# A two-layer SSD/HGRN2/PEER trunk on one core: queries projected before their norm's root is known, and the final norm taken on token rows

## The reference

```
def rmsnorm(x, g):
    r = lax.rsqrt(jnp.mean(xf * xf, axis=-1, keepdims=True) + NORM_EPS)
    return (xf * r).astype(x.dtype) * g

for layer in range(DEPTH):                      # DEPTH = 2
    h = rmsnorm(x, mix_norm_g[layer])
    x = x + (ssd_mixer if layer == 0 else hgrn2_mixer)(h, ...)
    h = rmsnorm(x, ffn_norm_g[layer])
    x = x + peer_ffn(h, w_query, sub_keys, u, v)
return rmsnorm(x, final_norm_g)

# peer_ffn: q = h @ w_query (2048 columns); scores q . sub_keys; top 16 of each half,
# top 16 of their sums, softmax gates; out = sum over chosen experts of gate * gelu(h . u) * v
```

## Time and profile before

| | |
|---|---|
| median of three runs | 2242.07 us |
| profiled execution, its own time | 2241.06 us |
| its span | 2239.3 us |
| PE busy | 2111.5 us (94%) |
| ACT, DVE, POOL busy | 1105.0, 1126.4, 1160.8 us |
| mean granted clock of PE | 0.98 |

### The profile page before, as it was taken

One profiled execution on the slowest core, in us unless ns is written; L12 is line 12 of the kernel. 1 busy time (PEld: TensorE's weight loads), 2 busy tenths in 40 slices (PEclk: granted clock), 3 DMA queues, 4 the chain that ended last, 5 costly groups with the idle time before them and its releaser, 6 DMA issues.

```text
span 2239.3 us, 42069 instructions
## 1 busy us (share of the span) xinstructions
PE 2111.5 (94%) x14527; PEld 1942.0 (87%) x14530; DVE 1126.4 (50%) x1760; ACT 1105.0 (49%) x1693; POOL 1160.8 (52%) x584
## 2 busy tenths in 40 slices
PE   6987799999999999999988988999999999999998
PEld 5986799999999878888878978999999987888886
DVE  5867419990002854444445841899200086444444
ACT  4654354445445655545445444544454465454553
POOL 0162568898885044554520006799888703545552
PEclk9998999999999999999999989999999999999999
DMA  4531445555563055565533334555566404555552
GB/s 144 165 122 50 150 150 169 178 168 194 184 197 110 1 188 192 193 194 192 194 130 132 114 105 132 158 168 167 181 196 197 159 1 134 195 190 194 193 193 102
DMA packets 103887, 345.71 MB, mean 154 GB/s; under 512 B 18704, under 2 KB 20240, under 8 KB 103440
## 3 DMA queue, kind: packets, MB, share of 16 engines
q1 hardware_dynamic: 94512, 340.67, 46.5%
q10 hardware_dynamic: 9312, 4.19, 1.0%
HBM read 341.68 MB, written 3.15 MB: 154 GB/s over the span
## 4 chain that ended last, share of the span: by engine, by line
PE 48%; issue 30%; POOL 20%; DVE 1%; POOLq 0%; ACT 0%; DVEq 0%; ACTq 0%
PE banks L1076 31%; POOL wlo L411 20%; PE banks L748 10%; PE banks L1056 6%; PE banks L1037 1%; POOLq L410 0%; POOLq L415 0%; PE banks L791 0%; DVE x L1644 0%; DVE big L1110 0%; DVE big L1639 0%; DVE big L1609 0%; POOL hlo L440 0%; DVE raw L1618 0%; POOL big L425 0%
## 5 line engine op out<-in xcount | busy, mean ns | idle before, releaser
L411 POOL TENSOR_TENSOR wlo<-raw,whi 128x1024 fp32r<-128x1024 f32 x320 | 805.1, 2522 | 535.2 <-ACT whi L452 534.3
L748 PE MATMUL banks<-hhi,whi 128*128 128x256 f32 x3072 | 882.2, 287 | 62.9 <-DVE hlo L1120 26.4
L748 PE MATMUL banks<-hlo,whi 128*128 128x256 f32 x3072 | 875.7, 285 | 0.0
L748 PE MATMUL banks<-hhi,wlo 128*128 128x256 f32 x3072 | 875.1, 285 | 0.0
L452 ACT ACTIVATE whi<-raw 128x1024 fp32r<-128x1024 f32 x640 | 675.6, 1056 | 388.4 <-PE banks L1076 339.3
L748 PEld LDWEIGHTS banks<-hhi,whi 128*128 128x128 f32 x3072 | 596.1, 194 | 71.0 <-issue 48.3
L440 POOL TENSOR_TENSOR hlo<-big,hhi 128x256 fp32r<-128x256 f32 x256 | 351.7, 1374 | 505.9 <-ACT hhi L712 505.9
L748 PEld LDWEIGHTS banks<-hlo,whi 128*128 128x128 f32 x3072 | 596.4, 194 | 0.1
L748 PEld LDWEIGHTS banks<-hhi,wlo 128*128 128x128 f32 x3072 | 596.0, 194 | 0.0
L1632 DVE TENSOR_TENSOR wlo<-raw,whi 128x1024 fp32r<-128x1024 f32 x256 | 315.5, 1233 | 371.5 <-ACT whi L452 371.5
L1076 PE MATMUL banks<-whi,hhi 128*128 128x512 f32 x1024 | 316.8, 391 | 4.5 <-POOL hlo L440 4.5
(11 more groups left out here) (237 smaller groups left out, 1354.0 us busy)
## 6 DMA issues: line engine op xcount, KB each, us to landing
raw<-w_u SPq DMA_DIRECT2D x256, 512.0 KB, 3.5
raw<-w_v SPq DMA_DIRECT2D x256, 512.0 KB, 3.5
raw<-w_ssd_in SPq DMA_DIRECT2D x40, 512.0 KB, 3.5
raw<-w_q SPq DMA_DIRECT2D x32, 512.0 KB, 3.5
raw<-w_hgrn_in SPq DMA_DIRECT2D x32, 512.0 KB, 3.5
raw<-w_ssd_out SPq DMA_DIRECT2D x16, 512.0 KB, 3.5
raw<-w_hgrn_out SPq DMA_DIRECT2D x8, 512.0 KB, 3.5
big<-keys SPq DMA_DIRECT2D x2, 1024.0 KB, 7.5
```

The source lines that it names most:

```text
L411: nc.gpsimd.tensor_tensor(wlo[:, r, :, :], raw[:, r, :, :], whi[:, r, :, :].bitcast(F32), ALU.subtract).then_inc(lo_pool, 1)
L748: ins = nc.tensor.matmul(out, w[:, r, k, :], h[:, k, :], start=start and n == 0, stop=stop and n == 3 * KC - 1, **kw)
```

## The change

1. Queries. The first operand of q is no longer the normed hn: ACT makes hhi = g·x (scaled_hi, eight instructions of 256 columns) and DVE hlo = g·x − hhi (scaled_lo, eight), both without the root. PE computes q tiles 0 and 1, then the mean of the squares (norm), then the other tiles. DVE takes each q tile out of its bank with a multiplication by rstd, in place of ACT's copy, and makes hn (norm_scale) in between, one block each at tiles 4 to 11; ACT and DVE split hn at the end of q, for u. In layer 0 the additions of the mixer's output (add_acc) are interleaved with scaled_lo. The norm's PSUM bank of layer 0 moves from 3 to 7.
2. Value products. In contract the products with hhi of both token blocks come first, then, behind the wait for clo, those with hlo.
3. Final norm. In layer 1 clear() is replaced by 16 matmuls that put x, transposed, into banks 4 to 7, so that the value products are added to it. After v1 the squares and their sums over a row are taken from the banks (three of the four by ACT with an accumulator, one by DVE), the root is one number per partition, ACT and DVE scale the rows while they copy them to vt, PE transposes, and ACT and DVE apply g into fin, which four DMAs of 256 KB store.

```
+            def scaled_hi(n, ready, values):
+                for k in range(KC):
+                    if k % 2 == 0:
+                        act.wait_ge(ready, values[k // 2])
+                    nc.scalar.activation(hhi[:, k, :], x[:, k, :], ACT.Identity,
+                                         scale=par_at("norm_g", n * KC + k)).then_inc(hhi_done, 1)
...
+                act.wait_ge(mm_done, FIRST[f"q{layer}"])
+                scaled_hi(1 + 2 * layer, *ready)
+                for t in range(COUNT[f"q{layer}"]):
+                    hi(FIRST[f"q{layer}"] + t + 2, (t + 2) % RAW)
+                    if t == 1:
+                        squares(*ready)
+                        root(1 + 2 * layer)
+                act.wait_ge(mm_done, FIRST[f"u{layer}"])
                 acts_hi(hn, hn_done, 4 * layer + 3, 4 * layer + 4)
-                stream(f"q{layer}", copy_to(lambda t: col(t + SCRATCH0)))
...
+                project(f"q{layer}", 0, rs=range(2))
                 norm(1 + 2 * layer)
-                project(f"q{layer}")
+                project(f"q{layer}", 0, rs=range(2, RAW))
+                project(f"q{layer}", 1)
...
-                clear()
+                if layer == 0:
+                    clear()
+                else:
+                    for b in range(NB):
+                        for k in range(KC):
+                            nc.tensor.matmul(bank[4 + 2 * b + k // 4][:, P * (k % 4):P * (k % 4 + 1)],
+                                             x[:, k, b * P:(b + 1) * P], ident[:, :], start=k % 4 == 0, stop=True,
+                                             skip_group_check=True)
...
+            dve.wait_ge(mm_done, FIRST["q0"])
+            add_acc(0)
+            for b in range(4):
+                if b < 3:
+                    add_acc(b + 1)
+                scaled_lo(1, "q0", range(2 * b, 2 * b + 2))
...
+                norm_root(1 + 2 * layer)
+                for t in range(COUNT[f"q{layer}"]):
+                    dve.wait_ge(mm_done, FIRST[f"q{layer}"] + t + 1)
+                    nc.vector.tensor_tensor(q_t[:, t, :], bank[t % BANKS][:, 0:T], rstd[:, :],
+                                            ALU.mult).then_inc(evac, 1)
+                    if 4 <= t < 4 + KC:
+                        norm_scale(1 + 2 * layer, [t - 4])
+                acts_lo(hn, f"u{layer}")
...
+            for n in range(3):
+                b, e = divmod(n, 2)
+                nc.scalar.activation(fsq[:, b, 512 * e:512 * (e + 1)], bank[4 + n][:, :], ACT.Square,
+                                     accum_out=ssq[:, b, e:e + 1]).then_inc(fin_sq, 1)
             nc.scalar.preload_act_table(ACT.Sqrt)
-            norm(4, x_done, range(9, 13))
+            act.wait_ge(fin_ms, 1)
+            nc.scalar.activation(frs, frs, ACT.Sqrt).then_inc(fin_sd, 1)
+            act.wait_ge(fin_rs, 1)
+            for e in range(2):
+                nc.scalar.activation(vt[:, 0, 512 * e:512 * (e + 1)], bank[4 + e][:, :], ACT.Identity,
+                                     scale=frs[:, 0:1]).then_inc(fin_a, 1)
```

More of the change, by code:

```diff
@@ L85, with filled @@
 NCON = 3 + len(LEVELS)
-ACTS = {"ssd_in": 1, "y0": 2, "y1": 3, "q0": 4, "hgrn_in": 5, "hgrn_out": 6, "q1": 7}
+FILL = {}
+_at = 0
+for _n, _c in [("ssd_in", 2), ("y0", 2), ("y1", 2), ("q0", 8), ("u0", 2), ("hgrn_in", 2), ("hgrn_out", 2),
+               ("q1", 8), ("u1", 2)]:
+    FILL[_n] = _at, _c
+    _at += _c
+def filled(name, k=KC - 1):
+    at, n = FILL[name]
+    return at + k * n // KC + 1
 SCRATCH0 = 72
@@ L479, in col, with squares @@
                 return big[:, bass.ds(t, 1), :].rearrange("p a b -> p (a b)")
-            def norm(n, ready, values):
+            def squares(ready, values):
                 for b in range(4):
@@ L1069, in contract @@
                         pe.wait_ge(chi, 128 * layer + RAW * i + r + 1)
-                        pe.wait_ge(clo, 128 * layer + RAW * i + r + 1)
-                        for b in range(NB):
-                            tok = slice(b * P, (b + 1) * P)
-                            for c, ws in ((hhi, (whi, wlo)), (hlo, (whi,))):
+                        for c, ws in ((hhi, (whi, wlo)), (hlo, (whi,))):
+                            if c is hlo:
+                                pe.wait_ge(clo, 128 * layer + RAW * i + r + 1)
+                            for b in range(NB):
+                                tok = slice(b * P, (b + 1) * P)
                                 for w in ws:
@@ L1081, in _ @@
                     contract(i)
-                for b in range(NB):
-                    pe.wait_ge(vt_c, NB * layer + b + 1)
+                if layer == 0:
+                    for b in range(NB):
+                        pe.wait_ge(vt_c, b + 1)
                 for n in range(4):
+                    if layer == 1 and n % 2 == 0:
+                        pe.wait_ge(fin_a, n // 2 + 1)
+                        pe.wait_ge(fin_v, n // 2 + 1)
                     for j in range(2):
@@ L1102, in step, with norm_root @@
                 dve.wait_ge(own, count[0])
-            def norm(n, split=True):
+            def norm_root(n):
                 dve.wait_ge(ms_done, n + 1)
@@ L1108, in norm, with norm_scale @@
                 step(nc.vector.reciprocal(rstd[:, :], rstd[:, :]))
-                for k in range(KC):
+            def norm_scale(n, ks=range(KC)):
+                for k in ks:
                     ins = nc.vector.scalar_tensor_tensor(out=hn[:, k, :], in0=x[:, k, :],
@@ L1646, in _ @@
-            norm(4)
+                if layer == 0:
+                    for e in range(2):
+                        ins = nc.vector.tensor_copy(vt[:, 0, 512 * e:512 * (e + 1)], bank[4 + e][:, :])
+                    ins.then_inc(vt_c, 1)
+                    for n in range(4):
+                        dve.wait_ge(vt_mm, n + 1)
+                        v = x[:, 2 * n:2 * n + 2, :]
+                        nc.vector.tensor_tensor(v, v, bank[n][:, :].rearrange("p (m t) -> p m t", m=2),
+                                                ALU.add).then_inc(x_done, 1)
```

122 lines of the change are left out of this document (80 added, 42 removed).

## The result

The changed kernel takes 2216.0 us (median of 4 runs, 2214.3 to 2216.1), the kernel before 2239.7 (median of 4, 2237.2 to 2243.4). The ratio is 0.9894, 95% interval [0.9881, 0.9906]: 23.7 us less, faster. Four more runs of the changed kernel later gave 2215.5 to 2219.5, with the ratio 0.9893 [0.9878, 0.9908].

What follows compares the result with a forecast made beforehand. PE bounds the kernel, busy 2111.5 of 2239.3 us, so waits can win about 128. Terms 6.2 + 6.8 + 0.6 + 1.1 + 4.4 = 19.1 off 2241.06 gave 2222.0; own range 2218 to 2226, wide 2216 to 2231.

Steps and rivals of the forecast that it cites:

- Queries: q0 and q1: tiles 0 and 1 start before the norm's root; 6.2 us less in layer 0, 6.8 in layer 1.
- The clock term: q0, tile 0: sparse matmuls may lower PE's clock; 1.1 us taken off the 7.3 gain, between 0 and 1.7.
- the means: PE's means of the squares between q tiles 1 and 2, taken as 3.72 us.
- Nothing waits: q0 behind the two early tiles: rstd frees the banks by 279.6, tile 4 wants one at 281.7; weights 1.3 us early.
- both sides of the port: DVE operations with two SBUF inputs and POOL operations reading SBUF exclude each other; multiplications out of PSUM banks do not.
- rival 2: Both q stages: DVE's multiplications out of banks also wait for POOL, PE waits 15.7 us a layer; 2253 us, chance 0.03.
- a low clock in q0's tiles for longer than 3 us: In the changed profile's q0, named as one sign that the forecast would be wrong.
- Rival 1: Both q stages: POOL's weight splits hold DVE's scaled_lo, 2.4 to 9.5 us more; 2224 to 2232 us, chance 0.16.
- The start of v0: PE begins v0's products once wlo is ready, without waiting for the first low half: 0.6 us less.
- v1: Start of v1: matmuls with x take 3.6 us, losing 0.6; the low-clock stretch goes, worth 1.7; net 1.1 us less.
- The tail: Behind v1, final norm on rows: end at 2234.9 against 2239.3, 4.4 us less, with transposes at half clock.
- Rival 4: No clock loss in q0, quicker scaled_hi, full-clock transposes: 3.3 us more off, perhaps 1 for stores; 2218.7 or 2217.7, chance 0.12.

Runs made afterwards that it cites:

- The first part alone: The kernel before with only the change to the queries: 2227.9 us, ratio 0.9938.
- the margin was taken away: The changed kernel with the weights of q tile 2 split on ACT ahead of the scaled rows, not behind: 2225.1 us, ratio 0.993.
- zeros on the first part: Kernel before with only the query change, plus matmuls on zeros: seven ahead of v0 and v1, thirteen ahead of the attention matmuls: 2221.5 us, ratio 0.9913.
- the third part: The kernel before with only the final norm on token rows changed: 2234.9 us, ratio 0.9977.
- the second part: The kernel before with only the order of the value products changed: 2235.9 us, ratio 0.9978.
- Work that fills waits everywhere: The changed kernel with matmuls on zeros at five places where PE waits, and the Sqrt table loaded before v1 ends: 2217.1 us, ratio 0.9898.

## Why the prediction was right and where it fell short

In short: the mechanisms of all three parts came as forecast, and the sum missed 6 us. The step that failed is the account of PE's clock. The sum gave v0 nothing for it and HGRN2 no term at all, without a reason for either; the runs showed 1.6 us less in v0 and 3.7 less in HGRN2, and 1.1 more than forecast lost in the gates of layer 1.

**Queries: right, sizes a little low.** 6.2 and 6.8 were forecast. The first part alone brought 6.5 and 7.2, and in the changed kernel it is 6.7 (7.3 less 0.6 for the shorter wait at v0) and 7.2. The clock term was nearly right: tile 0 of layer 0 ended 7.0 us behind the first addition to x, where the forecast without a clock term had 6.2, and with six matmuls on zeros ahead of it it ended 0.7 earlier. Windows from the start of tile 0 to the means, layer 0 and layer 1, show the granted clock at 0.79 and 1.00:

```profile
264.80:272.75 7.95, 7.55 (x49) 7.34 (x50) 3.83 (x9) 6.33 (x12) 3.74 (x2) 0.79 0.06 6
1332.80:1338.88 6.08, 6.08 (x49) 6.08 (x49) 2.63 (x7) 6.05 (x12) 2.98 (x2) 1.00 0.01 3
```

What was too dear in both layers was the means: 3.26 us up to tile 2 and not 3.7, which is most of the difference. ACT's scaled rows came every 0.41 us (8 in 3.31) and not every 0.46, but tile 0 of layer 1 ended only 0.15 earlier by it. "Nothing waits" behind the two tiles was right, as were both sides of the port: the 32 multiplications out of a bank took 0.41 to 0.43 us each and were free of it, so rival 2 did not happen. One of the forecast's signs of being wrong, a low clock in q0's tiles for longer than 3 us, did appear by a little: the matmuls from 266.2 to 269.2 run at half pace, and it cost no more than the term had.

**Rival 1 did not happen, by 0.4 us.** The forecast had a margin of 0.3 and 0.5 us and the trace has 0.4 and 0.5. When the margin was taken away, one low half was held in layer 0 and two in layer 1, 7.5 us in all with ACT's delay, inside the 2.4 to 9.5 forecast for it. The rule of the Trainium skill cited in the prediction agrees with these rows.

**The start of v0: right in the wait, wrong in what the wait carries.** The forecast took 0.6 us for the shorter wait, and it is 0.6 (2.26 to 1.66). But it used the stretch at 0.67 clock behind v1's idle time for v1 alone. v0 had the same 2.26 us ahead of it, and shortening it to 1.66 took out the same stretch, 1.6 us. This is the first half of the step that failed: a price that was read for one place was not applied to its twin, because there the idle time only shrank. Zeros in that wait, with nothing else changed, took the stretch out of both v stages, and with zeros on the first part it went again. A wait of 2.26 us is not the whole cause: the third part's v0 had it and lost nothing.

**HGRN2: a term that was missing.** This is the second half, and the larger. The sum counted only stages that the change edits. Beyond v0 stand 200.5 us in which PE waits several times for 3 us and more, and there the clock falls in some profiles and not in others. That is 3.7 us, 2.9 of it the attention matmuls (8.40 to 5.53). In the kernels with the old queries about 2.5 of it came back, 1.0 ahead of the end of u1 and 1.5 in layer 1's gates; in the changed kernel the gates gave back 1.1 more than forecast. The row for this was in the forecast, read as the price of an idle time of 3.35 us; after the change the same idle time costs nothing:

```profile
1288.09 0.46 PE L1038 MATMUL banks<-big 128*128 128x128 f32 x2 [3.34 <-ACT big L678]
1288.39 0.39 PE L1039 MATMUL banks<-big 128*128 128x128 f32 x2
```

The Trainium skill ("TensorE: Matmul & The Clock Gate", "What's actually happening") says that the block which watches PE runs freely and does not start anew with the kernel, so that it matters where in it work falls. The third part's profile fits that: it has the instructions of before up to the end of u1 in layer 1, and gets there 3.5 us earlier. The two profiles of the changed kernel do not speak for it: they are 2.3 us apart from the start on and have the same stretches. That this is the reason is not shown, and what decides in HGRN2 is not settled.

**v1: right, in both halves.** 3.6 us of matmuls with x were forecast and took 3.5 (1851.11 to 1854.60); the stretch at half clock went, 1.6 for 1.7. The stage ahead of v1 lost 1.7 us and not 0.6; over it the granted clock is 0.98 where it was 1.00.

**The tail: right in its order and nearly so in size.** 11.9 us were forecast and are 11.1. The squares end 1.84 us behind v1 (forecast 1.9), with the accumulator read free of cost at 0.2 beside the next square; the scaled rows reach PE at 4.5 (4.4). The transposes ran mostly at half clock as forecast, 3.14 for 16 where 3.4 was taken (3.03 to 3.65 in the five profiles that have them behind 4.5 us of idle time, 1.94 where zeros fill it). A store landed 2.1 us after its issue, not 2.75, by the list of DMA issues after (KB each, median from issue to landing):

```profile
out_t<-big SPq DMA_DIRECT2D x4, 256.0 KB, 2.1
```

**Rival 4 came nearest in time, by luck.** It had 2217.7 to 2218.7 by full clock in q0 and in the transposes, quicker scaled rows and a shorter store. Half clock fell in both places; of its terms the shorter store came (0.6 of 1), and the scaled rows gave 0.15.

By sizes, 25.1 against 19.1: the clock in v0, HGRN2 and the gates 4.2, the queries with the start of v0 0.9, the tail 0.8, the start of the kernel 0.3, v1 -0.1, together 6.1, for the 6.0 that were missing, since the terms are rounded.

**The parts seem to add up, and do not quite.** Their three ratios multiply to 0.9893, beside 0.9894 for the whole. But the second and the third part, each alone, both took the half clock out of v0 and out of HGRN2, and the changed kernel can gain that only once: by the profiles the three gains are 14.3, 5.2 and 8.1, 27.6 us together against 25.1. That the ratios agree is partly accident. Of the second part's 5.2 us, 1.2 are its own waits (0.6 at each v stage) and 4.0 the clock, and zeros ahead of v bring about as much with no edit to the order.

## What to carry to other kernels

Where the trace shows a stretch at lower clock behind an idle time, look for every other place with an idle time of that length and price it too, even if the change only shortens it. And take the price of a group of matmuls from its start to the start of what follows, not from the duration shown. Give stages behind the change that have idle times of their own a term with both signs (here 4 us in 200), or measure a version with zeros in the wait first: it costs a line and tells how much of a gain is the clock. Work that fills waits everywhere was no remedy here, since half clock then fell elsewhere; at the end, behind which nothing follows, it saved 1.2 us by the trace (with the table load moved), which the times alone do not show.

## What was not expected of the hardware

- 1.6 us hang on 0.6 us of idle time: a v stage took 350.05 behind 2.26 us without work in eight of nine cases (348.44 in the ninth) and 348.45 behind 1.66 or less in all nineteen.
- The same instructions up to u1 ended at 1790.96, 1791.59 and 1787.45 us (before twice, third part).
- Reading ACT's accumulator took 0.19 to 0.21 us beside a 0.60 us square, and starts overlapped it: three squares with their reads took 1.84 us.
